# Three x pieces beside the first weight chunk, the other five and the natural x behind it

## The reference, cut to what matters

```python
x = layer_norm(ALPHA * x + 0.5 * swiglu(x, ffn1_w_up, ffn1_w_down), ln1_g, ln1_b)
h, new_buf, S_new = mixer(x, ...)          # one wide projection, short convolution, retention, merge
x = layer_norm(ALPHA * x + h, ln2_g, ln2_b)
x = layer_norm(ALPHA * x + 0.5 * swiglu(x, ffn2_w_up, ffn2_w_down), ln3_g, ln3_b)
# swiglu(x) = (silu(a) * b) @ w_down, with [a | b] = x @ w_up, D_FF = 2816
```

## Time and profile before

| | |
|---|---|
| median of 3 runs | 1887.28 us (1886.36 to 1888.89) |
| the profiled execution | 1886.21 us, its span 1884.4 us (1.8 us lie around the span) |
| busy share of PE, DVE, ACT, POOL | 96%, 67%, 33%, 31% |
| DMA | 286.80 MB, mean 152 GB/s |
| granted clock of PE, mean | 0.984 |

### The profile page before, as it was taken

The page is one execution under the profiler, slowest core; times in us unless marked ns, Lnnn a source line. Parts: engine busy times, 40 slices in busy tenths (PEclk is TensorE's granted clock), DMA queues, the critical chain, the costliest instruction groups (busy, mean ns, idle before and its releaser), DMA issues. The chain is left out here.

```text
span 1884.4 us, 26852 instructions
## 1 busy us (share of the span) xinstructions
PE 1805.5 (96%) x10900; PEld 1676.7 (89%) x10900; DVE 1267.0 (67%) x1635; ACT 614.3 (33%) x1038; POOL 577.8 (31%) x378
## 2 busy tenths in 40 slices
PE   7999999997899999999999999999797999999996
PEld 6989899896899999999898898988777889899895
DVE  7768486577787778743667565665838767585666
ACT  4325233241444444410421405133104224243240
POOL 5324232232242222114323232331234323233230
PEclk9999999998999999999999999999898999999998
DMA  8332423304543334258457484765754333324312
GB/s 296 127 128 79 135 86 117 134 23 157 179 134 118 118 109 130 70 183 299 156 199 251 157 310 162 240 228 215 269 198 150 123 103 104 129 71 131 123 45 101
DMA packets 88314, 286.80 MB, mean 152 GB/s; under 512 B 8704, under 2 KB 11136, under 8 KB 87680
## 3 DMA queue, kind: packets, MB, share of 16 engines
q1 hardware_dynamic: 40832, 151.80, 24.9%
q10 hardware_dynamic: 29792, 69.32, 9.9%
q0 software_dynamic: 17568, 63.97, 9.8%
HBM read 247.76 MB, written 37.30 MB: 151 GB/s over the span
## 5 line engine op out<-in xcount | busy, mean ns | idle before, releaser
L525 POOL TENSOR_TENSOR wl<-raw,wh 128x1024 fp32r<-128x1024 f32 x122 | 319.3, 2619 | 100.1 <-DMA wh<-in_weights 88.6
L602 PE MATMUL ps<-th,wql 128*128 128x320 f32 x1040 | 321.3, 309 | 0.5 <-ACT pu L996 0.5
L602 PE MATMUL ps<-th,wqh 128*128 128x320 f32 x1040 | 321.1, 309 | 0.0
L602 PE MATMUL ps<-tl,wqh 128*128 128x320 f32 x1040 | 320.6, 308 | 0.0
L516 POOL DMA_DIRECT2D wh<-in_weights x122 | 68.3, 560 | 691.9 <-PE ps L602 630.9
L1354 DVE TENSOR_TENSOR wql<-qraw,wqh 128x512 fp32r<-128x512 f32 x195 | 242.4, 1243 | 24.9 <-ACT wqh L996 24.9
L996 ACT ACTIVATE pu<-ps 128x320 f32<-128x320 f32 x195 | 85.4, 438 | 506.8 <-PE ps L602 506.8
L602 PE MATMUL ps<-xh,wql 128*128 128x320 f32 x780 | 240.6, 308 | 3.3 <-DVE mv L1538 1.9
L602 PE MATMUL ps<-xl,wqh 128*128 128x320 f32 x780 | 240.5, 308 | 0.0
L602 PE MATMUL ps<-xh,wqh 128*128 128x320 f32 x780 | 240.5, 308 | 0.0
L1354 DVE TENSOR_TENSOR wql<-quad_s,wqh 128x512 fp32r<-128x512 f32 (+1 forms) x195 | 180.5, 925 | 55.5 <-ACT wqh L996 55.1
(11 more groups left out here) (180 smaller groups left out, 3753.9 us busy)
## 6 DMA issues: line engine op xcount, KB each, us to landing
qraw<-in_quads SPq DMA_DIRECT2D x130, 512.0 KB, 3.6
raw<-in_weights SPq DMA_DIRECT2D x122, 512.0 KB, 3.8
wh<-in_weights POOLq DMA_DIRECT2D x122, 512.0 KB, 5.0
state<-in_state_ret ACTq DMA_DIRECT2D x48, 512.0 KB, 7.5
out_ret_sample<-state ACTq DMA_DIRECT2D x32, 512.0 KB, 5.1
qk_scratch<-ctp SPq DMA_DIRECT2D x8, 640.0 KB, 5.5
z_scratch<-z ACTq DMA_DIRECT2D x1, 2560.0 KB, 7.5
z<-gate_c_scratch SPq DMA_DIRECT2D x4, 640.0 KB, 6.4
```

The costliest lines, as they stand in the source:

```text
L525: pool.tensor_tensor(wl[:, r, :], raw[:, r, :], wh[:, r, :].bitcast(f32), ALU.subtract).then_inc(chunk_split, 1)
L602: ins = nc.tensor.matmul(out, lhs, rhs, start=start, stop=stop, skip_group_check=adds)
```

## The change

SP asks for raw of chunk 0 first, then pieces 0 and 2; it waits until wh of chunk 0 has landed (`hi_loaded[0]`), then asks for pieces 4 and 6 and raw of chunk 1, without a wait for piece 3. ACT asks for piece 1, waits for the same landing, then asks for pieces 3, 5 and 7; the eight copies stand behind that. POOL no longer waits for piece 3 before it asks for wh of chunk 1. The two loads of the natural x into z leave ACT's start and are issued in `window`, behind the four `th` copies. No arithmetic changes.

```diff
--- before.py
+++ after.py
@@ -424,14 +424,13 @@
                 sync.dma_start(xin[:, f, c], a["x_T"][:, f, c]).then_inc(x_in[n], 16)
 
             def ffn(k):
+                load(1)
                 if k == 0:
                     load_x(0)
-                load(1)
-                if k == 0:
                     load_x(2)
+                    sync.wait_ge(hi_loaded[0], 16)
                     load_x(4)
                     load_x(6)
-                    sync.wait_ge(x_in[3], 16)
                 load(1)
                 if k == 0:
                     sync.wait_ge(x_in[7], 16)
@@ -548,8 +547,6 @@
                 if k == 1:
                     high(ck(3))
                 low()
-                if k == 0:
-                    pool.wait_ge(x_in[3], 16)
                 high(ck(1))
                 if k == 0:
                     pool.wait_ge(x_in[7], 16)
@@ -1037,6 +1034,9 @@
             def window(ffn):
 
                 x_hi_parts(2 * ffn)
+                if ffn == 0:
+                    act.dma_start(z[:, 0:PT, :], a["x_prompt"].rearrange("(t p) d -> p t d", p=128)).then_inc(z_in, 16)
+                    act.dma_start(z[:, PT, :], a["x_sample"]).then_inc(z_in, 16)
                 n = QUAD_START[2 * ffn]
                 b = full(2)
                 result(nc.scalar.activation(two(sig[:, :]), pair(b), ACT.Sigmoid))
@@ -1132,6 +1132,8 @@
                         result(copy(xh[:, part[0], part[1]], x))
 
             for n in range(1, len(X_PIECES), 2):
+                if n == 3:
+                    act.wait_ge(hi_loaded[0], 16)
                 half, ks = X_PIECES[n]
                 c, f = slice(half * HALF, (half + 1) * HALF), slice(ks[0], ks[-1] + 1)
                 act.dma_start(xin[:, f, c], a["x_T"][:, f, c]).then_inc(x_in[n], 16)
@@ -1139,8 +1141,6 @@
                 c, f = slice(half * HALF, (half + 1) * HALF), slice(ks[0], ks[-1] + 1)
                 act.wait_ge(x_in[n], 16)
                 result(copy(xh[:, f, c], xin[:, f, c]))
-            act.dma_start(z[:, 0:PT, :], a["x_prompt"].rearrange("(t p) d -> p t d", p=128)).then_inc(z_in, 16)
-            act.dma_start(z[:, PT, :], a["x_sample"]).then_inc(z_in, 16)
             act.dma_start(ident[:, :], a["ident"]).then_inc(consts_in, 16)
             act.dma_start(odd_even[:, :], a["odd_even"]).then_inc(consts_in, 16)
             act.dma_start(convw[:, :, :], a["conv_w"]).then_inc(cache_in, 16)
```

## The result

| | before | changed |
|---|---|---|
| median of 14 runs each | 1887.74 us (1883.61 to 1889.84) | 1891.97 us (1889.01 to 1893.56) |
| ratio, with its 95% interval | | 1.0022 (1.0014 to 1.0030) |
| the profiled execution, its span | 1886.21, 1884.4 us | 1891.74, 1889.9 us |
| start of the first product with quad weights (**the marker**) | 60.75 | 66.59 |
| from the marker to the span's end | 1823.7 | 1823.3 |

The change costs 4.2 us in the median, 5.5 us between the two profiled executions. The forecast was 2.6 us. In the profiled executions all of it lies ahead of the marker, which is 5.84 us later; the rest is the same to 0.4 us. So the marker is the measure of this study: it leaves out what the other 1820 us add to the scatter.

What follows compares the result with a forecast made beforehand. The prediction took PE's start to be bound by DVE and POOL taking turns up to `hl`. 1886.21 (profiled) + 2.6 = 1888.8; that execution lies 1.07 under the median, so 1889.9 us; range 1885.6 to 1893.

Steps and rivals of the forecast that it cites:

- port chain: DVE and POOL taking turns from the last x piece's split to `hl`; claimed to start later, +2.6 us.
- `hl` as the last wait: PE's wait for `hl` of the second plain tile decides the end; `hl` at 52.7, PE resumes at 52.75.
- rival (c): wh of chunk 3 behind z: load takes 9.8 us, PE idles 6.8, clock falls; +4.95 us, 1892.2; chance 0.20.
- likeliest case: The forecast itself: 2.6 us slower, 1889.9 us on the median; chance 0.45.
- T: Landing of wh of chunk 0 in the changed kernel, put at 7.7 us instead of 8.55.
- byte count: Ahead of wh of chunk 0, 2.03 MB asked for instead of 2.30 moved; the missing 0.27 MB are 0.7 us.
- (b): Wh of chunk 0 gets no earlier, T stays 8.55; port chain +3.4 us, 1890.7; chance 0.15.
- (a): Early chunk, small gain: wh lands at 6.25, piece 7 at 12.35, port chain 1.4 us sooner; 1885.9; chance 0.15.
- ACT's wait: Wait before three x issues, table load and copies; PE starts 1.35 us later, at 12.4, costing nothing at the end.
- SP's wait and piece 7: DMA engines run dry about 2 us behind SP's wait; piece 7 lands at 16.3 instead of 12.7.
- I take 7.0: Load time in us of wh of chunk 3 beside z: asked for about 30.5, landing 37.5, split until 40.1.
- So it adds nothing: PE waits 4.0 us before unit 3, ends chunk 4's first half at 50.8, before 52.75; zero cost.

Runs made afterwards that it cites:

- e4: The changed kernel with 36 extra products that nobody reads, between unit 2 and unit 3, filling PE's wait; ratio 1.0020 to the kernel before.
- e9: The changed kernel with z asked for only behind the last quad weight copy; ratio 1.0014 to the kernel before.
- e1: The changed kernel with the two z loads put back ahead of the small constants; ratio 1.0025 to the kernel before.
- e5: The changed kernel without ACT's wait for wh of chunk 0, SP's wait kept; ratio 1.0005 to the kernel before.
- e11: The changed kernel with the copies of pieces 0, 1 and 2 and the table load ahead of ACT's wait; ratio 1.0024 to the kernel before.
- e6: The changed kernel without SP's wait for wh of chunk 0, ACT's wait kept; ratio 1.0019 to the kernel before.
- e3: The kernel before with z asked for only behind the last quad weight copy; ratio 1.0001 to the kernel before.
- e10: The kernel before with ACT's wait for wh of chunk 0 alone, the two waits for piece 3 taken out; ratio 1.0006 to the kernel before.
- e8: The kernel before with z behind the last quad weight copy and wh of chunk 3 asked for ahead of the quad sums; ratio 0.9979 to it.
- e12: The kernel before with only wh of chunk 3 asked for ahead of the two quad sums, z where it was; ratio 1.0003 to it.

## Why the prediction was right, and where it was off

The direction and the range (1885.6 to 1893) held: 1891.97 lies in it. The mechanism held as far as POOL's quad sums: late x pieces start the port chain late. Behind them it did not. The forecast had `hl` as the last wait and named it a sign of being wrong if it were not; in the changed kernel it is not, and the last wait is for chunk 3, as in rival (c). The likeliest case, 1889.9, was 2 us low on the median, and the measured 0.22% is just past the line of 0.2% that the text drew, on the side to which it gave 0.25. That the median lies between the forecast and (c), though the profiled execution goes beyond (c), is in part luck.

- **Chunk 0.** T was put at 7.7; it is 7.75. The closeness is in part luck: the load took 6.5 us in e4 too, but 6.7 in e9 and 7.2 in e1, which start with the same code, so T is 7.75 to 8.45, against 8.35 to 8.75 in the five runs that start as the kernel before. The byte count points the right way, and e1 comes near (b), whose T was 8.55. (a) did not come. The gain hangs on ACT's wait: with SP's alone (e5) the load took 7.5 us.
- **ACT's wait.** First product put at 12.4, found at 12.37, released by `xl`. That the late first product costs nothing by itself is shown by e11.
- **SP's wait and piece 7.** Put at 16.3, found at 17.3. The engines did run dry (60 GB/s from 8 to 10 us), and once more from 17 to 18 (0 GB/s), which the working had not: raw of chunk 2 and the quads wait for piece 7 too. e6 shows that without SP's wait the x sums start only 1.5 us sooner (19.74), held by ACT's late copies, which the working did not price apart.
- **The port chain.** The order was right: the split of chunk 1 at 18.17 ahead of the last `xl` part, no wait before chunk 1. The end of the quad sums was put at 30.5 and is 31.52; the 1.0 us is piece 7's.
- **z.** This is the step that failed: "I take 7.0" and, after it, "So it adds nothing". That path, over chunk 3, had 1.95 us to spare (50.8 against 52.75), and its 4.0 us of waiting had no price for the clock: behind the waits of 3.32 us (e3) and 4.09 us (e10) the clock was 0.66 over 5 us, which is 1.7 us. Three errors of one sign used them up: the sums end 1.0 us later, the load takes 1.1 us longer, the split 3.05 us instead of 2.6, together 2.5; the fallen clock, 2.79 us, comes on top. The sum closes: 2.6+2.5+2.79-1.95 = 5.9, measured 5.84. wh of chunk 3 took 8.1 us to its split (with z issued only at 29.15, 1.2 us later than I had it), PE waited 6.09 us instead of 4.0. That is rival (c), whose point was a landing of 7.4 us: unit 3 ended at 52.6 and not 47.1, `hl` followed it instead of leading. What removing z alone brings is small (e9), since `hl` is late as well. Rival (c)'s price was put at 4.95 us over the kernel before and the marker is 5.84 us later in the profile; its clock term was put at 1.5 us and measures 2.79 (e4), because the clock stayed at 0.50 through 22 products.
- **What e9 adds.** The forecast's own path, `hl` at 52.7, was real: with z away `hl` comes at 53.77 and ends the last wait.
- **Not settled.** The median grew by 4.2 us, the profiled execution by 5.5. Executions of one kernel differ: DVE and POOL take turns in another order from one to the next. In e3 the split of chunk 1 took 3.74 us; the earlier trace rows has 6.49. The z move is not the cause: e8 moves z as well and there the two splits of chunks 1 and 2 take 9.78 us, as DVE's first two x sums go first (2.88 us; 5.10 in e3):

```profile
15.27 3.74 POOL L525 TENSOR_TENSOR wl<-raw,wh 128x1024 fp32r<-128x1024 f32 x1 [2.06 <-DMA wh<-in_weights]
```

The clock may fall in some and not in others; no run shows it. Which share of the 4.2 us is clock was not found.

## What to carry to other kernels

A wait put in front of loads also holds whatever stands behind it on that engine: here ACT's wait held the copies of pieces that had long come, and with them a table load, which cost more than the at most 0.8 us won on the first chunk. Before delaying bytes, ask what the DMA engines will do in the meantime and which later load the displaced bytes will meet; of the three places tried for z, the start, behind the x sums, and after the last load that PE waits for, the last was the best, and only with that load asked for earlier (e8); by itself it gained nothing (e3). When an edit moves one of two late chains, look for the other before calling the first harmless.

## What was not expected of the hardware

- PE's waits of 5 to 6 us at the start are followed by a granted clock of 0.50, and so are those of 2.87 us (e5), 3.32 (e3) and 4.09 (e10), for less long. In e9 two waits of 2.50 and 1.70 us with 0.96 us of work between them had the same effect (0.58 from 53 to 60 us), while single waits of 1.1 to 1.7 us in the kernel before had none, nor had those of 2.04 (e8) and 2.08 us (e12).
- The clock column does not show everything: the first 20 products of the kernel before (21 of the changed) stand 267 ns apart, as at 1.2 GHz elsewhere, though it says 1.00 there (11 to 16 us of the kernel before, 18 products):

```profile
11.00:16.00 5.00, 4.96 (x18) 4.96 (x19) 5.00 (x7) 2.73 (x4) 1.74 (x3) 1.00 1.07 401
```

- When DVE's two-input operations follow each other without a gap, POOL's split can wait for several of them (6.49 us in the earlier trace rows, three x sums long) or for one (3.74 in e3); where it starts in a gap it takes 2.42, and DVE's `xl` part beside it 3.16 instead of 0.81. The Trainium skill, "SBUF — State Buffer", section "SBUF: two separate sides", tells of an exclusive pair that the one who is first holds for the instruction; the traces agree that the two take turns.
- The same load of 512 KB takes 4.3 us from issue to split (e9) or 8.1 (changed), where the two kernels differ only in where z is asked for.
